# Row groups normed one stage earlier, projection weights split one stage earlier, and a shorter decision in a bitwise search, in a two-layer decoder trunk

## The reference

```python
# layer A: an indexer scores keys, each query keeps its 256 best
score = einsum('bqh,bqhl->bql', w_idx, relu(q_idx . k_idx)); score = where(causal, score, -inf)
_, sel = top_k(score, 256)
# end of a layer: projection, RMSNorm, gated residual
y = (o * silu(gate)) @ w_out
x = x + res_gate * rms_norm(y, post_g[i])
# start of the next layer
h = rms_norm(x, pre_g[i]) * (1.0 + scale) + shift
proj = h @ w_in            # layer B: q, k, v and gate, 4 x 1024 columns
```

## Time and profile before

| what | value |
|---|---|
| median of 3 runs | 3811.56 us (3802.57 to 3811.91) |
| profiled execution, own time | 3815.45 us |
| its span | 3813.8 us |
| PE busy | 3443.9 us, 90% |
| DVE busy | 2136.0 us, 56% |
| ACT busy | 2016.5 us, 53% |
| POOL busy | 523.0 us, 14% |
| mean granted TensorE clock | 0.943 of full speed |

### The profile page before, as it was taken

One profiled execution on the slowest core, in us unless ns is written; L12 is line 12 of the kernel. 1 busy time (PEld: TensorE's weight loads), 2 busy tenths in 40 slices (PEclk: granted clock), 3 DMA queues, 4 the chain that ended last, 5 costly groups with the idle time before them and its releaser, 6 DMA issues. The chain is left out here.

```text
span 3813.8 us, 65226 instructions
## 1 busy us (share of the span) xinstructions
PE 3443.9 (90%) x18786; PEld 2572.1 (67%) x18786; DVE 2136.0 (56%) x5870; ACT 2016.5 (53%) x3490; POOL 523.0 (14%) x550
## 2 busy tenths in 40 slices
PE   5879898888999999998977999999888888889799
PEld 3756454476666666666856888889866666666687
DVE  3669999995555555655644111000087777777344
ACT  2558899946777777774223111111166666666222
POOL 2000355001111111110220111121020000000011
PEclk8989999978999999998988999999999999999889
DMA  8661789563222232224542444222232222221442
GB/s 237 181 148 26 220 238 238 167 229 94 80 75 83 82 80 75 81 76 169 174 142 89 117 122 122 77 77 67 76 111 66 70 67 70 70 67 34 142 139 100
DMA packets 430046, 436.41 MB, mean 114 GB/s; under 512 B 81792, under 2 KB 341280, under 8 KB 429600
## 3 DMA queue, kind: packets, MB, share of 16 engines
q1 hardware_dynamic: 417984, 429.65, 38.3%
q10 hardware_dynamic: 11872, 4.46, 1.0%
HBM read 271.44 MB, written 162.53 MB: 114 GB/s over the span
## 5 line engine op out<-in xcount | busy, mean ns | idle before, releaser
L1387 DVE CUSTOM_DVE_ANT_0 a_att_sb_lg<-a_att_ps_s,mask 128x512 f32<-128x512 f32 (+3 forms) x512 | 302.5, 596 | 217.3 <-PE a_att_ps_s L1279 176.5
L1453 ACT ACTIVATE b_att_sb_lg<-b_att_sb_lg,b_att_sb_negm 128x384 f32<-128x384 f32 (+15 forms) x256 | 305.6, 1198 | 127.0 <-DVE b_att_sb_negm L1395 126.8
L1285 PE MATMUL b_att_ps_s<-b_att_sb_k,b_att_sb_q 64*128 64x512 f32 (+3 forms) x1920 | 294.8, 418 | 85.6 <-DVE b_att_sb_lg L1389 71.4
L1461 ACT ACTIVATE a_att_sb_pT<-a_att_ps_t 128x512 f32<-128x512 f32 (+3 forms) x640 | 316.0, 530 | 104.6 <-PE a_att_ps_t L1298 97.8
L1453 ACT ACTIVATE a_att_sb_lg<-a_att_sb_lg,a_att_sb_negm 128x384 f32<-128x384 f32 (+15 forms) x256 | 307.3, 1201 | 78.6 <-DVE a_att_sb_negm L1395 78.6
L1298 PE MATMUL a_att_ps_t<-ident,a_att_sb_lg 128*128 128x128 f32 x2176 | 340.0, 279 | 0.0
L1389 DVE TENSOR_SCALAR_CACHE_REDUCE b_att_sb_lg<-b_att_ps_s 128x512 f32<-128x512 f32 (+3 forms) x512 | 282.9, 590 | 98.5 <-PE b_att_ps_s L1285 78.1
L1815 DVE TENSOR_SCALAR_CACHE_REDUCE mask<-scores,threshold_bits 128x384 bf16<-128x384 f32 (+8 forms) x288 | 322.6, 1187 | 1.2
L1298 PEld LDWEIGHTS a_att_ps_t<-ident,a_att_sb_lg 128*128 128x128 f32 x2176 | 248.7, 141 | 107.4 <-issue 57.4
L1278 PE MATMUL a_att_ps_s<-a_att_sb_k,a_att_sb_q 128*128 128x512 f32 (+3 forms) x640 | 287.3, 449 | 26.5 <-DVE a_att_sb_mx L1387 15.9
L1315 PE MATMUL a_att_ps_o<-a_att_sb_pT,a_att_sb_v 128*64 128x256 f32 (+1 forms) x2304 | 297.4, 377 | 0.2 <-DMA a_att_sb_v<-scratch_v 0.2
(11 more groups left out here) (302 smaller groups left out, 7020.9 us busy)
## 6 DMA issues: line engine op xcount, KB each, us to landing
a_att_sb_q<-scratch_qT SPq DMA_DIRECT2D x512, 64.0 KB, 2.5
select_sb_w_gate<-in_a_w_in SPq DMA_DIRECT2D x32, 512.0 KB, 5.4
mask_sb_mod_w<-in_mod_w SPq DMA_DIRECT2D x16, 1024.0 KB, 6.8
a_att_sb_k<-scratch_kT SPq DMA_DIRECT2D x128, 128.0 KB, 2.8
b_att_sb_q<-scratch_qT SPq DMA_DIRECT2D x128, 128.0 KB, 2.5
b_att_sb_k<-scratch_kT SPq DMA_DIRECT2D x64, 256.0 KB, 4.2
b_qkgv_sb_w<-in_b_w_in SPq DMA_DIRECT2D x30, 512.0 KB, 4.7
front_sb_mod_w<-in_mod_w SPq DMA_DIRECT2D x8, 1024.0 KB, 7.8
```

Of the source, the lines that this page charges most:

```text
L1285: mm = nc.tensor.matmul(s_ps[:, (n + m) % SR, 0:z - a], q[rows, p // 2 % QS, x, cols], k[rows, slot, y, a:z], start=(j == 0), stop=(j == 2))
L1387: x = nc.vector.tensor_tensor_reduce(out, src, tab, 1.0, 2 * NEG, sign, ALU.max, top[:, col:col + 1])
L1453: nc.scalar.activation(buf, buf, ACT.Exp, bias=negm[:, p, m:m + 1], accum_out=sums[:, b, ds(h * M + m, 1)]).then_inc(exp_done, 1)
L1461: nc.scalar.activation(pT[:, r % 2, a:z, c:c + P], t_ps[:, n % TR, 0:z - a], ACT.Copy).then_inc(t_left, 1)
```

## The change

It has three parts.

1. **Next rows normed in the output stage.** Two buffers lie at the far end of SBUF and live over both stages: `ahead.w` (the two first units' weights) and `ahead.x` (two groups of 512 rows, which is also the place of `a_out`'s unsplit output weights before). Behind group 5's stores SP issues four more loads: the two units' weights (512 KB each) and x1's row groups 0 and 1 (2 MB each). Between groups 6 and 7 ACT squares and roots row group 0, and DVE scales it. `b_in` then begins with PE's transposes and with POOL's splits, and neither loads nor norms row group 0. Row group 1 is in SBUF when the stage begins.
2. **`b_in` splits the next stage's first weights.** Each of the two weight buffers is loaded again when it was split, with the first two units of `b_qkgv`, and POOL splits them behind `b_in`'s last matmuls on each unit. `b_qkgv` takes over the buffers, gives its semaphores the counts of a finished pair, and its loads and splits begin with pair 1.
3. **Two operations for a decision.** `picked = cnt >= enough`, and `bits = (picked << bit) ^ flipped`. `flipped` is no longer made between `bits` and the first count, but behind the first count of the next pass, and nothing waits for it there.

The modulation's buffers lie at the far end too, and are freed before layer A's attention.

```diff
@@ stage_enter
+            for u in range(units):
+                sp.wait_ge(w_lo_done, u + 1)
+                sp.dma_start(w[:, u], next_weights(u)).then_inc(w_in, 16)
...
             for u in range(units):
-                pool.wait_ge(w_in, 16 * (u + 1))
-                nc.gpsimd.tensor_copy(w_hi[:, u], w[:]).then_inc(w_hi_done, 1)
+                nc.gpsimd.tensor_copy(w_hi[:, u], w[:, u]).then_inc(w_hi_done, 1)
                 pool.wait_ge(w_hi_done, u + 1)
-                nc.gpsimd.tensor_tensor(w_lo[:, u], w[:], w_hi[:, u], ALU.subtract).then_inc(w_lo_done, 1)
+                nc.gpsimd.tensor_tensor(w_lo[:, u], w[:, u], w_hi[:, u], ALU.subtract).then_inc(w_lo_done, 1)
+            for u in range(units):
+                pool.wait_ge(w_in, 16 * units)
+                pool.wait_ge(summed, (G - 1) * units + u + 1)
+                nc.gpsimd.tensor_copy(w_hi[:, u], w[:, u]).then_inc(w_hi_done, 1)
+                pool.wait_ge(w_hi_done, units + u + 1)
+                nc.gpsimd.tensor_tensor(w_lo[:, u], w[:, u], w_hi[:, u], ALU.subtract).then_inc(w_lo_done, 1)
...
-            act.wait_ge(eps_set, 1)
-            square(0)
             for k in range(KD):
                 leave_h(0, k)
+            act.wait_ge(eps_set, 1)
             square(1)
...
-            normalise(0)
             for k in range(KD):
                 split(0, k)
@@ stage_project
-            for u in range(2):
-                load(jobs[0], 0, u)
...
             pool.sem_inc(left, CREDIT)
+            for u in range(2):
+                pool.sem_inc(w_in[u], 16)
+            pool.sem_inc(w_hi_done, 2)
+            pool.sem_inc(w_lo_done, 2)
@@ stage_select
+            def flip(bit):
+                step(nc.vector.tensor_scalar(flipped[:], bits[:], 3 * 2 ** (bit - 2) if bit >= 2 else 1, None, ALU.bitwise_xor))
...
                 for place, i in enumerate(BY_DVE):
+                    if place == 1 and s:
+                        flip(bit + 1)
...
-                step(nc.vector.tensor_tensor(over[:], cnt[:], enough[:], ALU.subtract))
-                settle()
...
-                    step(nc.vector.tensor_scalar(picked[:], over[:], 0.0, float(2 ** bit), ALU.is_ge, ALU.mult))
+                    step(nc.vector.tensor_tensor(picked[:], cnt[:], enough[:], ALU.is_ge))
                     settle()
-                    nc.vector.tensor_tensor(bits[:], flipped[:], picked[:], ALU.bitwise_xor).then_inc(tried, 1)
+                    nc.vector.scalar_tensor_tensor(bits[:], picked[:], bit, flipped[:], ALU.logical_shift_left, ALU.bitwise_xor).then_inc(tried, 1)
                 dve.wait_ge(tried, s + 2)
-                if bit:
-                    step(nc.vector.tensor_scalar(flipped[:], bits[:], 3 * 2 ** (bit - 2) if bit >= 2 else 1, None, ALU.bitwise_xor))
-                    settle()
@@ stage_output
+            def load_ahead():
+                for u, weights in enumerate(ahead.weights):
+                    sp.dma_start(ahead.w[:, u], weights).then_inc(ahead_w_in, 16)
+                after(sp, w_lo_done, KD)
+                for j in range(2):
+                    after(sp, stored[j], 4 * 16)
+                for g in range(2):
+                    sp.dma_start(ahead.x[:, g], dst[g * 512:(g + 1) * 512, :].rearrange("(j p) n -> p j n", p=P)).then_inc(ahead_in, 16)
...
+            def square_ahead():
+                after(act, ahead_in, 32)
+                for j in range(4):
+                    after(act, y_squared, NG * 2 - 2)
+                    after(act, ahead_squared, j)
+                    nc.scalar.activation(ysq[:], ahead.x[:, 0, j], ACT.Square, accum_out=ass[:, j:j + 1]).then_inc(ahead_squared, 1)
+                after(act, ahead_squared, 4)
+                nc.scalar.activation(asd[:], ass[:], ACT.Sqrt, bias=eps[:], scale=1.0 / D).then_inc(ahead_rooted, 1)
...
+            def normalise_ahead():
+                after(dve, ahead_rooted, 1)
+                nc.vector.reciprocal(ars[:], asd[:]).then_inc(ahead_inverted, 1)
+                after(dve, ahead_inverted, 1)
+                for j in range(4):
+                    nc.vector.tensor_scalar(ahead.x[:, 0, j], ahead.x[:, 0, j], ars[:, j:j + 1], None, ALU.mult).then_inc(ahead_normed, 1)
```

More of the change, by code:

```diff
@@ L185, in _ @@
                 sp.wait_ge(stored[u], G * units // 2 * 32)
+            sp.wait_ge(w_in, 16 * units)
         @block.gpsimd
@@ L345, in units @@
             for c, job in enumerate(jobs):
-                with engine.Fori(0, job.pairs) as i:
+                ready = 1 if before_pair is not None and c == 0 else 0
+                with engine.Fori(ready, job.pairs) as i:
                     if before_pair is not None:
@@ L2056, in stage_output, with groups @@
         idle_sp = st.sem("idle_sp")
+        if ahead is not None:
+            ass, asd, ars = (st.sb(f"ahead_{n}", [P, 4], F32) for n in ("ss", "sd", "rs"))
+            ahead_w_in, ahead_in, ahead_squared, ahead_rooted, ahead_inverted, ahead_normed = (
+                st.sem(f"ahead_{n}") for n in ("w_in", "in", "squared", "rooted", "inverted", "normed"))
         block = st.block()
-        def groups(engine, step):
+        def groups(engine, step, near_end=None, last_two=None):
             with engine.Fori(0, NG // 2 - 1) as i:
@@ L2063, in groups @@
                 step(i * 2 + 1, 1, False)
+            if last_two is not None and ahead is not None:
+                last_two()
             step(NG - 2, 0, False)
+            if near_end is not None and ahead is not None:
+                near_end()
             step(NG - 1, 1, True)
@@ L2100, in _ @@
             load(1, 1, False)
-            groups(sp, step)
+            def load_ahead():
[6 more added lines that the diff above has]
+                    sp.dma_start(ahead.x[:, g], dst[g * 512:(g + 1) * 512, :].rearrange("(j p) n -> p j n", p=P)).then_inc(ahead_in, 16)
+            groups(sp, step, last_two=load_ahead)
             for j in range(2):
                 after(sp, stored[j], NG * 16)
+            if ahead is not None:
+                after(sp, ahead_w_in, 16 * len(ahead.weights))
+                after(sp, ahead_in, 32)
         @block.gpsimd
@@ L2331, in program @@
         stage_identity(nc, sems, ident)
[L2332 removed]
+        modulation = Modulation(lambda *a: far_sb(modulated, *a))
         held = ExitStack()
@@ L2347, in program @@
                 stage_mask(nc, sems, ins, scores, threshold, mask, modulation, ada, gp_dram)
+                modulated.close()
             sems.retire()
             stage_attention(nc, sems, "a_att", 16, 1, ident, bias_dram, qT, kT, v, oT, sums, mask=mask)
-        stage_output(nc, sems, "a_out", 1, ins["x"][0], x1, ins["a_w_out"][0], oT, gateT, gp_dram[0], sums, ident)
+        win = ins["b_w_in"][0].rearrange("(k p) n -> p k n", p=P)
+        early_w, early_x = ExitStack(), ExitStack()
+        ahead = Ahead(far_sb(early_w, "b_w", [P, ENTER, KD, P], F32), far_sb(early_x, "b_x", [P, 2, 4, D], F32),
+                      [win[:, :, u * P:(u + 1) * P] for u in range(ENTER)])
+        stage_output(nc, sems, "a_out", 1, ins["x"][0], x1, ins["a_w_out"][0], oT, gateT, gp_dram[0], sums, ident, ahead=ahead)
         sems.retire()
```

66 lines of the change are left out of this document (33 added, 33 removed).

## The result

The changed kernel took 3783.67 us in the median of 4 runs (3779.76 to 3784.43), against 3811.73 for the kernel before, run beside it (3802.57 to 3812.08): a ratio of 0.9923, 95% interval 0.9911 to 0.9935. That is 28.1 us faster; 3778.9 was forecast, in a range of 3769 to 3790. The profiled execution of after took 3779.76 us (span 3778.0), 35.7 less than the one of before: single executions of one kernel lie some 5 us to either side, and what of it is the change has to be read stage by stage.

What follows compares the result with a forecast made beforehand. Three engines near their limit, DVE nearest, bound the search; waits bound b_in. Savings of 10.8 (search), 15.3 (b_in) and 6.6 (b_qkgv) sum to 32.7 us: 3811.56 - 32.7 = 3778.9 us, range 3769 to 3790.

Steps and rivals of the forecast that it cites:

- Part 3, the pass: Search: DVE's pass falls from 10.96 to 10.62 us, by 0.34, with ACT level and the moved flip costing 0.08.
- The rival in which the flip costs a full step: Search: only 0.21 us saved a pass, 4 us less gain, 3783 us in all; chance 0.2.
- Part 3, the sum: Search: 9.2 us from 27 ordinary passes, 0.6 from three waiting ones, 1.0 from less POOL blocking; 10.8 us.
- Three waiting ones only `over`, 0.6: Search: the three passes where DVE waits for ACT save only the dropped `over` operation, 0.6 us together.
- 4.6 us in hand for PE: Search, passes 2 to 8: PE falls back 2.4 us in all but has 4.6 us to spare.
- Part 1: Start of b_in: PE transposes 17.3 us sooner, DVE's first split is held by POOL's weight splits; 15.3 us saved.
- Part 2: Start of b_qkgv: 8.1 us of load, cast and subtraction go, 1.5 us of POOL's semaphore increments come; 6.6 us saved.
- "nothing" for the clock: Start of b_qkgv: PE's slow start after a shorter idle is counted as no gain, though up to 1 us was possible.
- A search that doesn't shorten: Rival: ACT, PE and transfers are near their limits, a faster DVE only waits; search gains 0 to 2 us, 3789; chance 0.1.
- POOL that doesn't hold DVE: Rival at b_in's start: DVE gets its casts through beside POOL, up to 4.6 us more gain, 3774 us; chance 0.1.
- a moved split that isn't ready: Rival at b_qkgv's start: a moved split or load comes late, the third saving gives nothing, 3785 us; chance 0.03.
- late loads: Rival in a_out: added loads land late, costing from a landing at 1952 on, a loss from 1985 on; chance 0.03.

Runs made afterwards that it cites:

- e4: Changed kernel with the flip put back ahead of the first count, with its wait: 3780.57 us, run once for its trace.
- e5: Changed kernel with the flip left out from pass 12 on, so its threshold is another one: 3775.49 us, run once for its trace.
- e6: Changed kernel with four output buffers instead of three in the search stage, low halves keeping three: 3772.39 us, ratio 0.9893 to the kernel before.
- e0: The changed kernel itself, timed again in a second set of runs: 3784.76 us, ratio 0.9919 to the kernel before.
- e7: Changed kernel with POOL's splits of b_in's two weights moved into a_out, split weights at the far end: 3784.73 us, ratio 0.9922 to the kernel before.
- e1: Kernel before with only the two-operation decision and the flip behind the first count: 3806.57 us, ratio 0.9981 to the kernel before.
- e2: Changed kernel with the three-operation decision of before put back: 3793.40 us, ratio 0.9952 to the kernel before.

## Why the prediction was right, step by step

- *Part 3, the pass.* Right in each piece: 0.21 per operation that goes, 0.08 for the flip in its new place, 10.62 us a pass, with ACT level (e4, e5). The rival in which the flip costs a full step is out: it does so only in the chain. What the prediction quotes from the Trainium skill (VectorE: DVE Perf Modes, "The DRAIN you can't avoid"), that an operation starts only when the one before has drained, isn't what the flip does here: the count behind it starts 0.08 us after the flip's start though the flip lasts 0.17. The quotation left out that section's own exception. By the Trainium skill (VectorE: DVE Perf Modes, "Two Vector instructions with no wait between them") only a held instruction waits until every earlier one has finished; the 0.08 agrees with one that isn't held.
- *Part 3, the sum.* 8.7 instead of 10.8. The pass gave what was forecast, 30 x 0.34 = 10.2. Two terms were off. "Three waiting ones only `over`, 0.6" let DVE's waits for ACT grow by 0.4; they grew by 2.1 (9.0 to 11.1), of which pass 9's is new. The prediction looked whether DVE, ACT and PE could follow, with 4.6 us in hand for PE, and PE was never waited for; the buffer that is only free when its store has landed behind the loads of `h` stands in no term of the sum. With a fourth buffer (e6) DVE's waits fall to 3.4. And POOL's blocking went from 5.9 to 5.4, so 0.5 came back and not 1.0. 10.2 - 2.1 + 0.5 gives 8.6, the measured 8.7 but for rounding. The forecast's `bits` first to last was 333 us; it is 335.0, and 335.7 in e0.
- *Part 1.* 15.7 for 15.3. PE within 0.04 us of POOL's first operation, DVE held until POOL's second pair was over, no cost at `a_out`'s norms: all as said. That the numbers agree to 0.4 us is in part luck, since the stage scatters from 81.4 to 83.5. The end of the hold was forecast at 0.55 behind POOL's; DVE's cast that POOL's last operation held ended at 1968.72 for a POOL end at 1968.43, 0.3 behind, and one cast and subtraction more were through by then. The Trainium skill (SBUF — State Buffer, "SBUF: two separate sides") has the port pair that VectorE and GpSimd share as a lock, which the one that starts first holds for a whole instruction. The rows agree: DVE's 0.42 us cast ends at 1964.76, 0.28 behind POOL's first subtraction (1964.48), its subtraction at 1966.21, 0.55 behind POOL's second cast.
- *Part 2.* 6.6 for 6.6, and "nothing" for the clock holds: 664.5 to 665.9 us for `b_qkgv` whatever the gap (e7, with its buffers moved, apart).
- *The rivals.* A search that doesn't shorten is out (e1, e2), POOL that doesn't hold DVE too (e7), a moved split that isn't ready (7.25 us of idle), and late loads: the rows had landed at 1935.26, and the bound of 1952, moved by the 10.8 us that `a_out`'s last matmul came sooner, is 1941.
- *The total.* 8.7 + 15.7 + 6.6 = 31.0 in the stages that the change touches, less 0.3 behind `a_out`'s last matmul; 32.7 was forecast. The medians differ by 28.1, the interval is 25 to 34. The 3 us between them are within the scatter of stages that the change doesn't touch, and no loss that it causes is seen: `b_att` and `b_out` together took 1036.4 us before, 1035.2 after and 1042.4 in e0, and over all the profiled kernels 1028.7 to 1042.4, with the same instructions.

## What to carry to other kernels

When a loop's serial part is shortened, look at what doesn't come sooner with it: here a store that is issued on time but lands behind 2 MB of loads. One more buffer there was worth 7.1 us, nearly as much as the edit itself. Preparing the next stage's input under the last one pays twice, for the load and for the arithmetic, but check which engine then meets which at the new start: 4.3 of the norm's 9.5 us went to GpSimd's weight splits. A buffer that changes its place in memory is a change of its own; compare the duration of the instructions that read it. And compare stages between executions with like clock: executions of one and the same stage differed by up to 2 us along with it.

## What was not expected of the hardware

- The place of operands in the local memory changed the length of TensorE's matmuls: 391 to 392 ns with the split weights at the far end, 389 at the lower, 5 us over some 2100 such matmuls. Why is open; `a_out`'s own matmuls of the same shape have a median of 393 in every kernel.
- GpSimd's operations are stretched beside VectorE's too, but little: at the start of `b_in` one cast took 1.23 us where the other 23 of `b_in` and `b_qkgv` took 1.04, and one subtraction 2.69 where the others took 2.34 to 2.40. VectorE's went from 0.42 to as much as 2.59.
- `b_att` with the same instructions took between 792 and 804 us from one execution to another, which is the largest part of the scatter of the kernel's time.
